# Throwaway matrix products behind a finished transformer kernel: 936 products from shifted places, with seven column counts

## The chip, the cores and the metric

The kernel runs on one core of a Trainium2 chip. The metric is the device time of one execution in microseconds (us). A core has five engines that run side by side, each through its own list of instructions: TensorE (PE: matrix products, with the loads of their weights on a line of their own, PEld), VectorE (DVE), ScalarE (ACT), GpSimd (POOL) and SyncE (SP, which here only issues DMAs). They meet through semaphores. SBUF is the memory that TensorE reads from, PSUM the one it writes to, in eight banks.

## What is computed

Two transformer blocks over 512 tokens of 1024 features. The first has two gated feed-forward layers around a mixer of short convolution and gated linear attention, the second has neighbourhood attention, a retention layer and a feed-forward layer of width 4096. Cut to its outline:

```python
def first_block(x, ...):
    x = x + FFN_RES_WEIGHT * swiglu(rmsnorm(x, norm_ffn1_g[l]), ffn1_w_gu[l], ffn1_w_down[l])
    x = x + hybrid_mixer(rmsnorm(x, norm_mix_g[l]), w_in[l], conv_w[l], ...)
    x = x + FFN_RES_WEIGHT * swiglu(rmsnorm(x, norm_ffn2_g[l]), ffn2_w_gu[l], ffn2_w_down[l])
    return rmsnorm(x, final_norm_g)

def second_block(x, ...):
    ...
    x = x + mix @ w_out[l]
    h = rms_norm(x, norm_mlp[l])
    x = x + jnp.square(jax.nn.relu(h @ w_up[l])) @ w_down[l]
    return rms_norm(x, norm_final)
```

The output is the normed result, 512 x 1024 float32 values.

## The kernel before

The program is written engine by engine, with every semaphore wait by hand. Features lie on the 128 partitions, tokens along the free dimension. A large product is made of **units**: 128 output features by 512 tokens, summed over eight (or six) blocks of 128 input features. Each float32 operand is split in a high and a low part of type float32r, and each block takes three products: high weights by high data, high weights by low data, low weights by high data (L2064 to L2066 in `unit`). Some layers work on half the tokens at a time, with combined operands (`pair`, L2156 to L2158): these have 256 columns. TensorE reads the data (the moving operand, up to 512 columns) and the weights (128 columns) from SBUF.

The tiles that matter lie one behind the other in each partition of SBUF. `X` starts at byte 16512. `Hhi`, `Hlo`, `Ahi` and `Alo` (L304 to L307, 16 KB each: eight blocks of 512 float32r values) follow at bytes 32896, 49280, 65664 and 82048, then `raw`, `wh` and `wl` (12 KB each) at 98432, 110720 and 123008. All of these addresses are 128 bytes past a multiple of 1024. `BThi` and `BTlo` (28 KB each, seven by four blocks of 256 values) lie in a region `M` that starts at byte 162880, which is 64 bytes past a multiple of 1024, and `BTlo` starts 28 KB behind it, so again 64 bytes past one. `H*` and `A*` hold activations, `wh` and `wl` the split weights of the units in work (three slots of 1024 values each), `BK[i]` is PSUM bank i.

The end of the program is written out by hand in `pe_program` behind L2534. The last unit is made in two halves of 256 tokens (`products`, L2538 to L2540), while the two other engines form the mean squares of the last norm (`sums`, one-column products, L2544). Eight groups of four transposes (`turned`, L2550) turn the normed result back so that tokens lie on the partitions. DVE scales one half of each token block out of PSUM (L2022) and counts the semaphore `esd` up, ACT scales the other half (L1128) and counts `esa`. Each of the four token blocks gives one `esd` and one `esa`. SP issues the output DMAs as these counts rise (L486, L489), ACT the last one (L1141), and SP then waits until all eight have landed. At the end of the block all engines meet.

Of the kernel before, what the change touches and what calls it, by code (L numbers as in the profile page):

```python
# [14 lines left out]
P = 128  # L15
# [276 lines left out]
def build(nc, dr, out):  # L292
    at = [int(nc.sbuf_base)]

    def sb(name, shape, dt=F32, off=None):
        nb = 4 * int(np.prod(shape[1:]))
        if off is None:
            off = (at[0] + 31) // 32 * 32
            at[0] = off + nb
        t = nc.alloc_sbuf_tensor_at(name, list(shape), dt, offset=off)  # L300
        return t, off

    X, _ = sb("X", [P, KT, T])
    Hhi, oHhi = sb("Hhi", [P, KT, T], F32R)  # L304
    Hlo, oHlo = sb("Hlo", [P, KT, T], F32R)
    Ahi, oAhi = sb("Ahi", [P, KT, T], F32R)
    Alo, oAlo = sb("Alo", [P, KT, T], F32R)  # L307
    RAWS, _ = sb("raw", [P, NRAW, 1024])
    WHS, _ = sb("wh", [P, NW, 1024], F32R)
    WLS, _ = sb("wl", [P, NW, 1024], F32R)  # L310
# [63 lines left out]
    BTlo, _ = sb("BTlo", [P, NP, 4, 256], F32R, off=M + 28 * KB)  # L374
# [4 lines left out]
    BK = [PS[:, i, :] for i in range(8)]  # L379
# [73 lines left out]
    s = {}  # L453
# [2139 lines left out]
        turned(3, 1)  # L2593


    ctx = ExitStack()
    with ctx:
        s.update({n: ctx.enter_context(nc.semaphore(f"s_{n}")) for n in SEMS})
# [134 lines left out]
```

## Time and profile before

| | |
|---|---|
| median time of 2 runs | 1753.58 us (1753.15 to 1754.0) |
| span of the profiled execution, first to last instruction | 1751.3 us |
| PE busy | 1744.0 us (100%), 10407 products |
| PEld, weight loads | 1534.4 us (88%) |
| DVE busy | 1238.9 us (71%) |
| ACT busy | 850.4 us (49%) |
| read from HBM | 170.70 MB |
| mean granted TensorE clock | 0.999 |

Times in the profile count from the start of the span. A row of the timeline gives start, length, engine, source line, operation, the output and input tiles, and how many like instructions stand in the row. Products are pipelined, and the length shown for one contains its way through the array, so that neighbouring rows overlap: the pace of a stream is read from the distance of the starts, not from the length.

### The profile page before, as it was taken

Reading aid. Unit: us, or ns where it says so; the run is one execution under the profiler, and the core shown is the slowest. Engines: PE = TensorE matmul, PEld = TensorE weight load, DVE = VectorE, ACT = ScalarE, POOL = GpSimd, SP = SyncE. Lnnn points to the kernel's source line nnn. Section 1 sums busy time; section 2 is a strip of 40 time slices with the busy share of each in tenths; the row PEclk is TensorE's granted clock in tenths of the full one; section 3 lists DMA queues with packets and bytes.
Section 4 is the critical chain, followed back from the end, with each engine's and each line's share of the span. In section 5 each row is a group of like instructions: output and inputs, shape, how many; then the busy total and the mean of one; then the engine's idle time right before and its main releaser. Section 6 shows DMA issues by size and latency. Waiting matters only on the chain.

```text
span 1751.3 us, 26596 instructions
## 1 busy us (share of the span) xinstructions
PE 1744.0 (100%) x10407; PEld 1534.4 (88%) x10407; DVE 1238.9 (71%) x1955; ACT 850.4 (49%) x1442; POOL 38.8 (2%) x38
## 2 busy tenths in 40 slices
PE   9999999999999999999999999999999999999998
PEld 7889989878888899988888998988877888989897
DVE  7949849666776557965795894976688677748474
ACT  6425526454333335743553562654655543627274
POOL 0000000000000000000000000000232000000000
PEclk9999999999999999999999999999999999999999
DMA  5232423332123232333323233334511233333232
GB/s 185 82 109 97 127 89 104 110 110 85 51 86 106 86 108 97 109 111 98 96 88 117 93 110 96 109 109 131 141 61 61 85 96 97 97 96 118 89 120 72
DMA packets 68427, 176.61 MB, mean 101 GB/s; under 512 B 8112, under 2 KB 9392, under 8 KB 68304
## 3 DMA queue, kind: packets, MB, share of 16 engines
q1 hardware_dynamic: 66576, 171.60, 31.4%
q10 hardware_dynamic: 1280, 2.08, 0.3%
q8 instruction: 83, 1.36, 0.3%
q0 software_dynamic: 448, 1.24, 0.3%
q14 instruction: 40, 0.33, 0.1%
HBM read 170.70 MB, written 2.10 MB: 99 GB/s over the span
## 4 chain that ended last, share of the span: by engine, by line
PE 95%; DVE 3%; ACT 1%; issue 1%; DMA 0%; DVEq 0%; ACTq 0%; POOLq 0%
PE ps L2064 18%; PE ps L2066 18%; PE ps L2065 18%; PE ps L2156 10%; PE ps L2158 10%; PE ps L2157 10%; PE ps L2086 2%; PE ps L2087 2%; PE ps L2088 2%; DVE wl L1159 1%; PE ps L2305 0%; ACT BThi L579 0%; PE ps L2435 0%; DVE BTlo L1231 0%; PE ps L2460 0%
## 5 line engine op out<-in xcount | busy, mean ns | idle before, releaser
L2064 PE MATMUL ps<-Ahi,wh 128*128 128x512 f32 x913 | 357.2, 391 | 0.0
L2065 PE MATMUL ps<-Alo,wh 128*128 128x512 f32 x913 | 355.4, 389 | 0.0
L2066 PE MATMUL ps<-Ahi,wl 128*128 128x512 f32 x913 | 355.4, 389 | 0.0
L2156 PE MATMUL ps<-BThi,wh 128*128 128x256 f32 x1232 | 340.6, 276 | 0.3 <-ACT tm L569 0.3
L2157 PE MATMUL ps<-BTlo,wh 128*128 128x256 f32 x1232 | 340.3, 276 | 0.0
L2158 PE MATMUL ps<-BThi,wl 128*128 128x256 f32 x1232 | 340.2, 276 | 0.0
L543 ACT ACTIVATE wh<-raw 128x1024 fp32r<-128x1024 f32 (+1 forms) x206 | 213.1, 1036 | 221.6 <-PE ps L2066 187.4
L1159 DVE TENSOR_TENSOR wl<-raw,wh 128x1024 fp32r<-128x1024 f32 (+1 forms) x206 | 250.1, 1215 | 64.6 <-ACT wh L543 62.6
L2156 PEld LDWEIGHTS ps<-BThi,wh 128*128 128x128 f32 x1232 | 231.3, 188 | 0.6 <-issue 0.6
L2157 PEld LDWEIGHTS ps<-BTlo,wh 128*128 128x128 f32 x1232 | 231.3, 188 | 0.0
L2158 PEld LDWEIGHTS ps<-BThi,wl 128*128 128x128 f32 x1232 | 231.3, 188 | 0.0
L2066 PEld LDWEIGHTS ps<-Ahi,wl 128*128 128x128 f32 x913 | 171.4, 188 | 35.8
L2064 PEld LDWEIGHTS ps<-Ahi,wh 128*128 128x128 f32 x913 | 171.4, 188 | 35.7 <-issue 0.2
L2065 PEld LDWEIGHTS ps<-Alo,wh 128*128 128x128 f32 x913 | 171.4, 188 | 35.5 <-issue 0.2
L2064 PE MATMUL ps<-Hhi,wh 128*128 128x512 f32 x494 | 195.8, 396 | 0.0
L2066 PE MATMUL ps<-Hhi,wl 128*128 128x512 f32 x494 | 192.5, 390 | 0.0
L2065 PE MATMUL ps<-Hlo,wh 128*128 128x512 f32 x494 | 192.4, 390 | 0.0
L553 ACT ACTIVATE wh<-raw 128x512 fp32r<-128x512 f32 x168 | 105.2, 626 | 58.2 <-PE ps L2066 40.2
L1166 DVE TENSOR_TENSOR wl<-raw,wh 128x512 fp32r<-128x512 f32 x168 | 114.8, 683 | 2.7 <-ACT wh L553 1.6
L553 ACT ACTIVATE wh<-SS 128x512 fp32r<-128x512 f32 x112 | 70.7, 631 | 85.8 <-DVE SS L1182 78.2
L2064 PEld LDWEIGHTS ps<-Hhi,wh 128*128 128x128 f32 x494 | 92.8, 188 | 22.0 <-issue 3.1
L2066 PEld LDWEIGHTS ps<-Hhi,wl 128*128 128x128 f32 x494 | 92.7, 188 | 19.6
(355 smaller groups left out, 2707.7 us busy)
## 6 DMA issues: line engine op xcount, KB each, us to landing
raw<-in_w_gu SPq DMA_DIRECT2D x128, 256.0 KB, 2.8
raw<-in_w_d SPq DMA_DIRECT2D x32, 512.0 KB, 3.5
raw<-in_w_dn SPq DMA_DIRECT2D x32, 512.0 KB, 3.8
raw<-in_w_up SPq DMA_DIRECT2D x48, 256.0 KB, 2.8
raw<-in_w_gu SPq DMA_DIRECT2D x22, 512.0 KB, 3.6
raw<-in_w_d SPq DMA_DIRECT2D x16, 384.0 KB, 3.1
raw<-in_w_v SPq DMA_DIRECT2D x8, 512.0 KB, 3.8
raw<-in_w_cc SPq DMA_DIRECT2D x8, 512.0 KB, 3.6
```

The costliest lines, as they stand in the source:

```text
L543: act.activation(WH[WS[u]][:, 0:n], RAW[RSL[u]][:, 0:n], ACT.Copy).then_inc(s["wh"], 1)
L553: act.activation(WHP[WS[p][c]], part(p, c), ACT.Copy).then_inc(s["wh"], 1)
L1159: dve.tensor_tensor(WL[WS[u]][:, 0:n], RAW[RSL[u]][:, 0:n], f32(WH[WS[u]][:, 0:n]), ALU.subtract).then_inc(s["wl"], 1)
L1166: dve.tensor_tensor(WLP[i], part(p, c), f32(WHP[i]), ALU.subtract).then_inc(s["wl"], 1)
L2064: pe.matmul(ps, wh[:, c], hi[:, k, :], start=(k == 0), stop=False)
L2065: pe.matmul(ps, wh[:, c], lo[:, k, :], start=False, stop=False)
L2066: last = pe.matmul(ps, wl[:, c], hi[:, k, :], start=False, stop=(k == nb - 1))
L2086: pe.matmul(ps, Hhi[:, k, tc], wh[:, c], start=(k == 0), stop=False)
L2087: pe.matmul(ps, Hlo[:, k, tc], wh[:, c], start=False, stop=False)
L2156: pe.matmul(ps, whi[:, w], bhi, start=(new and kp == 0), stop=False, skip_group_check=not new)
L2157: pe.matmul(ps, whi[:, w], blo, start=False, stop=False, skip_group_check=not new)
L2158: last = pe.matmul(ps, wlo[:, w], bhi, start=False, stop=(kp == 3), skip_group_check=not new)
```

## The change

Behind the last transposes TensorE gets one more piece of program. It waits until DVE and ACT have scaled all four blocks (`esd` and `esa` at 4), and then runs `shifted` 78 times. Each call makes four times three products into the first n columns of PSUM bank 0, with the kernel's order of high and low parts. `at` and `step` say where in the flat moving tile the columns start (`at + step * n * k`), `at_w` where the 128 weight columns start. Nothing reads what these products leave in the bank. The output is not touched. No other engine's program changes, and nothing ahead of this piece changes.

```diff
@@ -2593,6 +2593,51 @@
         turned(3, 1)
 
 
+        def shifted(n, moving, at, weights, at_w, step=1, same=False):
+
+            hi, lo = ((t[:, :, :].rearrange("p a b -> p (a b)") if len(t.shape) == 3 else
+                       t[:, :, :, :].rearrange("p a b c -> p (a b c)")) for t in moving)
+            wh, wl = (t[:, :, :].rearrange("p a b -> p (a b)") for t in weights)
+            for k in range(4):
+                m, c = at + step * n * k, at_w + (0 if same else P * k)
+                for i, (w, x) in enumerate(((wh, hi), (wh, lo), (wl, hi))):
+                    pe.matmul(BK[0][:, 0:n], w[:, c:c + P], x[:, m:m + n], start=(k == 0 and i == 0),
+                              stop=(k == 3 and i == 2))
+
+        pe.wait_ge(s["esd"], 4)
+        pe.wait_ge(s["esa"], 4)
+        H, A, B, W, HW = (Hhi, Hlo), (Ahi, Alo), (BTlo, BTlo), (WHS, WLS), (Ahi, Alo)
+        for i in range(3):
+            shifted(512, H, 0, W, 0)
+        for at in (0, 1, 2, 4, 8, 12, 16, 20, 24, 32, 40, 48, 64, 80, 96, 112, 128, 192, 256, 384):
+            shifted(512, H, at, W, 0)
+        for at in (4, 8, 16, 32, 48, 64, 96):
+            shifted(512, H, 0, W, at)
+        for at in (8, 16, 32, 64):
+            shifted(512, H, at, W, at)
+        for at in (0, 16, 48, 112, 240):
+            shifted(512, B, at, W, 0)
+        shifted(512, A, 0, W, 0)
+        shifted(512, A, 16, W, 0)
+        shifted(512, H, 0, W, 0, 1, True)
+        shifted(512, H, 16, W, 0, 1, True)
+        shifted(512, H, 0, HW, 0)
+        shifted(512, H, 16, HW, 0)
+        shifted(512, H, 0, (Hhi, Hlo), 2048)
+        for at in (0, 4, 8, 16, 24, 32, 48, 64, 128):
+            shifted(256, H, at, W, 0)
+        for at in (0, 8, 16, 32, 48, 240):
+            shifted(256, H, at, W, 0, 2)
+            shifted(256, B, at, W, 0)
+        for at in (0, 16):
+            shifted(384, H, at, W, 0)
+            shifted(448, H, at, W, 0)
+            shifted(320, H, at, W, 0)
+            shifted(128, H, at, W, 0)
+            shifted(480, H, at, W, 0)
+        shifted(512, H, 0, W, 0)
+
+
     ctx = ExitStack()
```

On TensorE, at the end of its program, the order before the change is this (four transposes of `X` stand in each pair of rows; the last row is the jump to the place where all engines meet):

```order
L2550 MATMUL ps<-ident,X 128x128 [waits s_eacc,s_ex]
L2550 MATMUL ps<-ident,X 128x128 x3
L2550 MATMUL ps<-ident,X 128x128 [waits s_esd]
L2550 MATMUL ps<-ident,X 128x128 x3
L2597 UNCONDITIONAL_BRANCH
```

With the change the same place on TensorE reads as follows (output tile, then the moving tile and the weight tile, then partitions by columns):

```order
L2550 MATMUL ps<-ident,X 128x128 [waits s_esd]
L2550 MATMUL ps<-ident,X 128x128 x3
L2604 MATMUL ps<-Hhi,wh 128x512 [waits s_esa,s_esd]
L2604 MATMUL ps<-Hlo,wh 128x512
L2604 MATMUL ps<-Hhi,wl 128x512
```

The jump has moved behind 936 products, of which only the first waits for anything.

The list of TensorE now ends with the twelve products of the last call and the jump:

```order
L2604 MATMUL ps<-Hlo,wh 128x512
L2604 MATMUL ps<-Hhi,wl 128x512
L2604 MATMUL ps<-Hhi,wh 128x512
L2604 MATMUL ps<-Hlo,wh 128x512
L2604 MATMUL ps<-Hhi,wl 128x512
L2642 UNCONDITIONAL_BRANCH
```

By columns, the 936 products are 564 of 512 (47 calls), 252 of 256 (21 calls), and 24 each of 480, 448, 384, 320 and 128 (two calls each). Together they have 395,520 columns.

## Rows read from the trace of the kernel before

**Rows 1.** The page's head, its busy times, and its forty slices.
```profile
span 1751.3 us, 26596 instructions
...
PE 1744.0 (100%) x10407; PEld 1534.4 (88%) x10407; DVE 1238.9 (71%) x1955; ACT 850.4 (49%) x1442; POOL 38.8 (2%) x38
...
PE   9999999999999999999999999999999999999998
...
PEclk9999999999999999999999999999999999999999
```

**Rows 2.** The page's chain that ended last, by engine.
```profile
PE 95%; DVE 3%; ACT 1%; issue 1%; DMA 0%; DVEq 0%; ACTq 0%; POOLq 0%
```

**Rows 3.** Timeline around the end: start, length, engine, line, operation.
```profile
1744.23 2.38 PE L2550 MATMUL ps<-ident,X 128*128 128x128 f32 x20
...
1745.85 1.41 DVE L2022 TENSOR_SCALAR OT<-ps,rt 128x512 f32<-128x512 f32 x2
...
1746.28 1.26 ACT L1128 ACTIVATE OT<-ps,rt 128x512 f32<-128x512 f32 x2 [0.26 <-PE ps L2550]
...
1747.51 0.46 SPq L486 DMA_DIRECT2D out<-OT  x1
1747.57 0.36 ACTq L1141 DMA_DIRECT2D out<-OT  x1
```

**Rows 4.** Waits of the DMA queue of SP, 1742 to 1752 us.
```profile
SPq L2597 <- DMA out<-OT: 3.0, 1, 3.0
```

**Rows 5.** Timeline of PE at 566 us, 512 columns, first and last of 25.
```profile
566.21 0.39 PE L2064 MATMUL ps<-Ahi,wh 128*128 128x512 f32 x1
566.44 0.39 PE L2065 MATMUL ps<-Alo,wh 128*128 128x512 f32 x1
...
571.65 0.39 PE L2064 MATMUL ps<-Ahi,wh 128*128 128x512 f32 x1
```

**Rows 6.** Timeline of PE at 1115 us, 256 columns from BThi/BTlo, first and last of 37.
```profile
1114.77 0.28 PE L2158 MATMUL ps<-BThi,wl 128*128 128x256 f32 x1
...
1118.85 0.28 PE L2158 MATMUL ps<-BThi,wl 128*128 128x256 f32 x1
```

**Rows 7.** Timeline of PE at 1736 us, 256 columns from Ahi/Alo, first and last of 27.
```profile
1735.83 0.28 PE L2538 MATMUL ps<-Ahi,wh 128*128 128x256 f32 x1
...
1738.95 0.28 PE L2540 MATMUL ps<-Ahi,wl 128*128 128x256 f32 x1
```

**Rows 8.** Groups of PE by line and shape: count, busy us, mean ns.
```profile
L2064 PE MATMUL ps<-Ahi,wh 128*128 128x512 f32 x913 | 357.2, 391 | 0.0
...
L2064 PE MATMUL ps<-Hhi,wh 128*128 128x512 f32 x494 | 195.8, 396 | 0.0
...
L2550 PE MATMUL ps<-ident,X 128*128 128x128 f32 x32 | 3.9, 274 | 0.0
```

**Rows 9.** PE by stretches: length, PE busy (products), granted clock, DMA share, GB/s.
```profile
1742.56:1746.61 4.05, 4.05 (x38) 1.00 0.42 161
1746.61:1747.70 1.09, 0.01 (x1) 1.00 1.01 378
1746.61:1751.30 4.69, 0.01 (x1) 0.75 0.82 308
```

**Rows 10.** Timeline of PE at the program's start.
```profile
1.06 4.23 PE L2323 MATMUL ps<-ones 128*128 128x256 f32 x10 [1.06 <-DVE ones L1558]
```

**Rows 11.** Timeline of PE at 421 us.
```profile
421.36 1.46 PE L2293 MATMUL ps<-VT,KST 128*128 128x256 f32 x6
```

## The prediction

> **What bounds the kernel now.** I read the page's head first. TensorE is busy in 1744.0 of 1751.3 us, in every one of the forty slices, at the full granted clock [rows 1]. The chain that ended last is 95% TensorE [rows 2]. So the kernel is bound by the stream of products, and anything put into that stream lengthens it. The change puts its products behind the stream, so next I read the end of the timeline, for what may cover them.
>
> The last transposes end at 1746.61 (1744.23 + 2.38). DVE's last scaling ends at 1747.26 and ACT's at 1747.54, and the last two output DMAs are issued at 1747.51 and 1747.57 [rows 3]. SP then waits 3.0 us for the output to land [rows 4], and the span closes at 1751.3. In this stretch of some 3.7 us TensorE has nothing to do. That is all the cover there is.
>
> Last I read the pace of like products, from the distance of the starts. 512 columns: (571.65 - 566.21) / 24 = 0.2267 us each [rows 5]. 256 columns out of `BThi`/`BTlo`: (1118.85 - 1114.77) / 36 = 0.1133 us [rows 6]. 256 columns out of `Ahi`/`Alo`: (1738.95 - 1735.83) / 26 = 0.1200 us [rows 7]. The reader is to see two things. Between the 256 and the 512 columns of the A tiles lie 0.1067 us, which is one column per tick of 2.4 GHz, the level that a granted clock of 1.00 stands for. And each product pays something on top of its columns: 0.0133 us out of the A tiles, 0.0067 us out of the B tiles. The A tiles lie 128 bytes past a multiple of 1024, the B tiles 64 bytes past one. So the place of the data may change a product's price already in this kernel, by 0.0067 us. The calls of the change vary that place.
>
> **What the change removes, adds and moves.** Nothing is removed or moved: every row ahead of the new piece is the same on all engines. Added are two waits and 936 products, each with its own weight load. No DMA is added, and nobody waits for these products except the meeting of all engines at the end.
>
> *Start.* The wait for `esd` costs nothing by itself; the wait for `esa` ends last, with ACT's end at 1747.54. SP's DMA is issued 0.25 us after the DVE instruction that it waits for (1747.26 to 1747.51), so I let the first product start 0.16 us after ACT, at 1747.7; between 0.05 and 0.3 us the difference is nothing here.
>
> *The 564 products of 512 columns.* The same operation with the same operands as the kernel's own [rows 8], whose pace is 0.2267. Twenty-one of the 47 calls read from the kernel's own places or from ones a multiple of 128 bytes away; the others are shifted by 64 bytes more or by less than that. I can bound a shifted one from below by its columns alone, 0.2133, as in the last paragraph, and above by a product that pays twice the A tiles' surcharge, 0.2400, if reads that don't start on a round address take one more step. Between the two I take 0.226, a little under the A pace, since some calls shift into the place of the B tiles: 564 x 0.226 = 127.5 us. Bounds: 120.3 and 135.4 us.
>
> *The 252 products of 256 columns.* Fifteen of the 21 calls read `H`, which lies as the A tiles do, six read `B`, and shifts bring each into the other's place: 0.1200 and 0.1133 are both at hand, I take 0.116: 29.2 us. Bounds 0.1067 and 0.1333: 26.9 and 33.6 us.
>
> *The 24 each of 480, 448, 384 and 320 columns.* By the line through the A tiles' two paces (0.0133 + columns / 2400): 0.2133 + 0.2000 + 0.1733 + 0.1467 = 0.7333 us, times 24 = 17.6 us. Bounds 16.3 and 18.9 us.
>
> *The 24 of 128 columns.* The line would give 0.067 us. No row of the kernel shows a float32r product so short; the nearest is the transpose of 128 columns, twenty of them in 2.38 us with the way through the array [rows 3, 8], (2.38 - 0.27) / 19 = 0.111 us. A product that short may wait for its weights, which are 128 columns too. I take 0.11: 2.6 us; with 0.053 it is 1.3 us.
>
> Sum: 127.5 + 29.2 + 17.6 + 2.6 = 176.9 us. By the lower bounds 164.8 us, by the upper ones 190.5 us.
>
> *End.* The last product still needs its way through the array, about 0.16 us (a length of 0.39 less the pace of 0.23 [rows 5]), and then the engines meet. Before, that took from the landing (1747.97 + 3.0 = 1750.97) to 1751.3, 0.33 us. The output has landed long before, so the 3.0 us of its wait, which were the path of the end, drop out and are not paid.
>
> Span after: 1747.7 + 176.9 + 0.16 + 0.33 = **1925.1 us**. The median of the runs shown is 2.3 us above the span of the profiled execution (1753.58 - 1751.3), and the work around the span does not change: **1927.4 us**, 9.9% more than before. Put otherwise, 176.9 us of products, less 3.4 us that they share with the output's landing and the drain, plus the drain of their own.
>
> The notes state another pace. The Trainium skill, page "TensorE: Matmul & The Clock Gate", section "Back-to-back issue gap", gives a full-clock gap of columns / 2.4 GHz plus 2.5 ns for a single product, some 216 ns for 512 columns. By it the whole addition would be about 167 us and the time about 1918 us, an estimate from that page. The kernel's own rows are 11 ns above it at 512 columns, and the measurement decides.
>
> **The clock.** TensorE stands idle from 1746.61 to about 1747.7, and the granted clock in these 1.09 us is 1.00. Over the whole idle stretch to 1751.3 it is 0.75, so it fell to 0.5 (the 1.2 GHz level) about half way, near 1749.0, after some 2.3 us without work [rows 9]. With the change the idle time ends after 1.1 us. I cost the clock at nothing in the sum.
>
> **The rivals.**
>
> *The clock drops once at the start of the new piece* (0.12). For it: it did drop in this very stretch, if later, and before the gap there were only transposes and one-column products for 4 us. Against: it was at 1.00 all through these and the 1.1 us behind them. Price: at the program's start ten products take 4.23 us [rows 10], 0.42 us each; six of the same type and columns later take 1.46 us, under 0.25 us each with the last one's way through the array [rows 11]. That is a stretch of about 4 us at half pace, after which the pace is full, so one such stretch costs some 2 us: 1929.5 us. The skill's same page, section "Part 4: PE-mode transpose", holds that transposes don't count as work in the way that products do. By it this rival would be the likelier case; the clock of 1.00 through 4.05 us of transposes speaks against it so far.
>
> *Reads from odd places cost much more* (0.08). If a start that is no multiple of 64 bytes made each product take twice its time, this would hit eleven of the 512-column calls (shifts of the data by 1, 2, 4, 8, 12, 20, 24 or 40 values, of the weights by 4 or 8, and of both by 8) and five of the 256-column ones: 132 x 0.2267 + 60 x 0.117 = 37 us more, 1964 us. If only starts off a multiple of 16 bytes did (shifts of 1 and 2), 24 x 0.2267 = 5.4 us more, 1933 us. Nothing in the profile is for it, since the kernel has no such read, and nothing is against it.
>
> *Shifted and shorter products run at the price of their columns* (0.06): 164.8 us of products in the place of 176.9, 1915.3 us. For it: the B tiles' surcharge is only half of the A tiles'. Against: no stream of float32r products in the kernel pays less than 0.0067 us.
>
> *The products do not reach the end: the time is not slower* (0.01). For this the addition would have to fit into the 3.7 us of idle time and 2% of the kernel, 35 us: under 39 us for 936 products, 0.041 us each, where the 512-column ones alone would have to stream their columns at five times the pace seen. It could only be if the products were left out, and the order of instructions has all 936 of them ahead of the jump to the meeting of the engines. Then it would be 1753.6 us.
>
> *The clock falls and stays down* (0.02), with 353.8 us of products: about 2104 us. The dense stream of 1744 us at 1.00 speaks against it.
>
> The forecast itself has the rest, 0.71, with its own range of 1920 to 1933 us.
>
> **How the numbers follow.** The predicted time is that of the likeliest case, 1927.4 us. The range has to leave out no more than 2 in 10 and take in the bounds of the unknown paces: 164.8 us of products gives 1915, 190.5 us gives 1941. The odd-place case at its dearest and the clock that stays down lie outside, with under 0.1 together. So 1915 to 1941. A measurement of this kernel can tell about 2% from no change (35 us); all cases but the one without products lie over 9% above. Slower by over 2%: 0.99; within 2%: 0.01; faster: 0.
>
> **What would show it.** In the profile after, everything up to 1747.5 us has its old times. A row of L2604 with 936 products follows, starting near 1747.7. The starts lie 0.227 us apart in the first 36 products, where nothing is shifted; if they lie 0.45 apart at first, the clock has dropped. The shifted calls lie within 0.213 to 0.240; a call with 16 values' shift at 0.220 would say that 64 bytes are what separates the A tiles' price from the B tiles'. SP's wait for the output is followed by one for TensorE of about 170 us. The prediction is wrong if shifts move the pace by more than a few per cent, if products of 128 columns are not near 0.11 us, or if a call's first product, which opens a new sum in the same bank, waits for the one before.

## The result, and the profile after

| | before | after |
|---|---|---|
| median time | 1753.58 us (2 runs) | 1930.26 us (2 runs, 1930.21 and 1930.3) |
| ratio | | 1.1008, 95% interval 1.0987 to 1.1029 |
| span of the profiled execution | 1751.3 us | 1928.4 us |
| forecast | | 1927.4 us, range 1915 to 1941 |

The change makes the kernel 10.1% slower, by 176.7 us. The page of the changed kernel has the busy products of TensorE grown by 936 and everything else as it was (compare [rows 1]):

```profile
span 1928.4 us, 28469 instructions
...
PE 1924.6 (100%) x11343; PEld 1689.5 (88%) x11343; DVE 1239.4 (64%) x1955; ACT 850.5 (44%) x1442; POOL 38.7 (2%) x38
```

Its timeline around the end of the old program (to compare with [rows 3]): start, length, engine, line, operation.

```profile
1744.19 2.38 PE L2550 MATMUL ps<-ident,X 128*128 128x128 f32 x20
...
1746.23 1.27 ACT L1128 ACTIVATE OT<-ps,rt 128x512 f32<-128x512 f32 x2 [0.26 <-PE ps L2550]
...
1747.53 0.36 ACTq L1141 DMA_DIRECT2D out<-OT  x1
...
1747.64 0.47 PE L2604 MATMUL ps<-Hhi,wh 128*128 128x512 f32 x1 [1.07 <-ACT OT L1128]
...
1927.78 0.39 PE L2604 MATMUL ps<-Hhi,wl 128*128 128x512 f32 x1
```

The piece starts 0.14 us after ACT's last end (1747.50), and its last product starts at 1927.78: 935 distances in 180.13 us. The waits of SP's queue now name TensorE where [rows 4] named the output (longest wait last in the row):

```profile
SPq L2642 <- PEq L2642: 175.5, 1, 175.5
```

Stretches of this trace in the form of [rows 9] (length, PE busy with its products, clock, DMA share, GB/s), the first at the program's start, the second about the gap, the third nearly all of the piece:

```profile
0.00:4.00 4.00, 2.94 (x7) 1.00 0.52 160
...
1746.50:1747.60 1.10, 0.07 (x1) 1.00 1.02 382
...
1747.60:1925.00 177.40, 177.36 (x923) 1.00 0.02 7
```

The clock column says nothing here. This trace holds no record of the granted clock, and the column prints 1.00 for the first 4 us too, in which the row of ten slow products from [rows 10] runs (4.32 us here). So the clock has to be read from the pace. The first distances of the piece are 306, 235 and 234 ns, and they settle at 227. A piece that starts at the 1.2 GHz level shows 592, 427 and 427 (further below, in an execution whose trace has the record). The clock did not fall here.

The paces come out of the timeline of TensorE after. The first rows here are the starts of the calls with shifts of the data of 0, 1 and 2 values, the last three those of the calls on `BTlo` with shifts of 0, 16 and 48:

```profile
1755.93 0.39 PE L2604 MATMUL ps<-Hhi,wh 128*128 128x512 f32 x1
...
1758.65 0.40 PE L2604 MATMUL ps<-Hhi,wh 128*128 128x512 f32 x1
...
1761.51 0.40 PE L2604 MATMUL ps<-Hhi,wh 128*128 128x512 f32 x1
...
1841.80 0.39 PE L2604 MATMUL ps<-BTlo,wh 128*128 128x512 f32 x1
...
1844.60 0.39 PE L2604 MATMUL ps<-BTlo,wh 128*128 128x512 f32 x1
...
1847.34 0.40 PE L2604 MATMUL ps<-BTlo,wh 128*128 128x512 f32 x1
```

Twelve products lie between neighbouring rows of a pair. Unshifted: (1758.65 - 1755.93) / 12 = 0.2267 us. Shifted by one value: 2.86 / 12 = 0.2383. `BTlo` as it lies: 2.80 / 12 = 0.2333. `BTlo` shifted by 16 values: 2.74 / 12 = 0.2283, and 0.2267 in its last seven. So place counts, and at 512 columns the B tiles' place is the dearer one, the reverse of [rows 6, 7] at 256. By columns, all of the piece:

| columns | products | measured us each | forecast us each | difference of the sums, us |
|---|---|---|---|---|
| 512 | 563 distances | 0.2308 | 0.226 | +2.7 |
| 256 | 252 | 0.1179 | 0.116 | +0.5 |
| 480 | 24 | 0.2216 | 0.2133 | +0.2 |
| 448, 384, 320 | 72 | 0.2031, 0.1744, 0.1465 | 0.2000, 0.1733, 0.1467 | +0.1 |
| 128 | 24 | 0.1073 | 0.11 | -0.1 |

### The profile page after: what moved, and what is told of

It reads as the page before. It is cut to its first block, busy times and chain, and to the rows that moved or that the text cites. A ratio compares the mean times of both kernels' runs of the same rounds, so it can differ in the third digit from the quotient of the medians.

```text
span 1928.4 us, 28469 instructions
## 1 busy us (share of the span) xinstructions
PE 1924.6 (100%) x11343; PEld 1689.5 (88%) x11343; DVE 1239.4 (64%) x1955; ACT 850.5 (44%) x1442; POOL 38.7 (2%) x38
## 3 DMA queue, kind: packets, MB, share of 16 engines
q1 hardware_dynamic: 66576, 171.60, 28.3%
## 4 chain that ended last, share of the span: by engine, by line
PE 95%; DVE 3%; ACT 1%; issue 1%; DMA 0%; DVEq 0%; ACTq 0%; POOLq 0%
PE ps L2064 16%; PE ps L2065 16%; PE ps L2066 16%; PE ps L2604 9%; PE ps L2156 9%; PE ps L2158 9%; PE ps L2157 9%; PE ps L2086 2%; PE ps L2088 2%; PE ps L2087 2%; DVE wl L1159 1%; PE ps L2305 0%; ACT BThi L579 0%; PE ps L2435 0%; DVE BTlo L1231 0%
## 5 line engine op out<-in xcount | busy, mean ns | idle before, releaser
L2158 PEld LDWEIGHTS ps<-BThi,wl 128*128 128x128 f32 x1232 | 231.2, 188 | 0.0
L553 ACT ACTIVATE wh<-raw 128x512 fp32r<-128x512 f32 x168 | 105.1, 625 | 58.1 <-PE ps L2066 40.2
L2065 PEld LDWEIGHTS ps<-Hlo,wh 128*128 128x128 f32 x494 | 92.8, 188 | 19.5 <-issue 1.0
```

What stands on the lines that cost most here:

```text
L553: act.activation(WHP[WS[p][c]], part(p, c), ACT.Copy).then_inc(s["wh"], 1)
L2065: pe.matmul(ps, wh[:, c], lo[:, k, :], start=False, stop=False)
L2158: last = pe.matmul(ps, wlo[:, w], bhi, start=False, stop=(kp == 3), skip_group_check=not new)
```

## The experiments

Unless it says otherwise, an experiment is the changed kernel with another piece at its end, run once with its profile; what differs is far below the 2% that single times tell, so the distances of the starts within the profile decide, and the times are beside them. The front of the program varies by up to 1.3 us between executions (the last twenty transposes start at 1744.13 in one and 1745.42 in another), so I compare from there.

### Is it the shifts, or the calls?

```diff
-        for i in range(3):
-            shifted(512, H, 0, W, 0)
-        for at in (0, 1, 2, 4, 8, 12, 16, 20, 24, 32, 40, 48, 64, 80, 96, 112, 128, 192, 256, 384):
-            shifted(512, H, at, W, 0)
...
+        for n, count in ((512, 46), (256, 21), (384, 2), (448, 2), (320, 2), (128, 2), (480, 2), (512, 1)):
+            for i in range(count):
+                shifted(n, H, 0, W, 0)
```

> The same 936 products with the same column counts, all read from the start of Hhi/Hlo and wh/wl (no shift of data or weights, no other tiles). Theory PLACE (a product's price follows from where its data lie relative to its weights): 512 columns at 0.2267 throughout, 256 columns at 0.1200, 564 x 0.2267 + 252 x 0.1200 + 20.2 = 178.3 us of products instead of the 180.1 us seen with the shifts, time 1928.4 us. Rival CALL (each call costs something when it opens a new sum in the same bank, whatever the place): as with the shifts, 180.1 us and 1930.3 us, and slower products at the head of each call of twelve.

Measured: 1929.43 us, span 1927.6 us, 178.56 us from the first start to the last (forecast 178.3, with the shifts 180.13). The distances are 227, 226, 227 ns in every call of 512 but the first and the last, over every call's head, and 120 ns in every call of 256 after the first. So a new sum in the same bank costs nothing, and the shifts cost 1.6 us in all: 2.2 us more in the products of 512 columns (127.8 us unshifted, 129.9 shifted) and 0.5 us less in those of 256 (30.2 and 29.7). Only the first eleven products after a change are irregular: 306, 235, 233, 236, 224, 231, 236, 228, 233, 231, 226, and then 227.

### What the cover of the idle time is worth

```diff
-        pe.wait_ge(s["esd"], 4)
-        pe.wait_ge(s["esa"], 4)
...
-                pe.matmul(BK[0][:, 0:n], w[:, c:c + P], x[:, m:m + n], start=(k == 0 and i == 0),
+                pe.matmul(BK[END[5]][:, 0:n], w[:, c:c + P], x[:, m:m + n], start=(k == 0 and i == 0),
```

> The changed kernel without the two waits ahead of the piece, its products going into the bank of the first transposes, which has been read by then. The piece starts right behind the last transposes, at 1746.6 instead of 1747.64. Theory: the piece is added end to end to the stream, so the time falls by the whole gap, 1.0 to 1.1 us, to 1929.2 us, and the slow products at the head of the piece (306, 235, 234 ns apart) are at 227. Rival: something else holds the start (the fetch of the new instructions), and the time stays at 1930.3 us.

Measured: 1929.64 us, span 1927.8 us. In its timeline the piece follows the transposes without a gap:

```profile
1744.93 2.38 PE L2550 MATMUL ps<-ident,X 128*128 128x128 f32 x20
1747.07 0.47 PE L2604 MATMUL ps<-Hhi,wh 128*128 128x512 f32 x1
1747.38 0.39 PE L2604 MATMUL ps<-Hlo,wh 128*128 128x512 f32 x1
```

From the start of the transposes to the end of the span it is 182.9 us, after the change 184.2 us: 1.3 us less, of which the gap is 1.07; the rest is that the first product now starts 0.24 us before the last transpose has come through the array (1744.93 + 2.38 = 1747.31). The piece is simply put end to end with the stream, as the forecast had it. Its slow head stays (the distances are 314, 229, 233, 236, 224, 231, 236), so that is no effect of the gap; the expectation was wrong there, and what makes the head stays open.

### What the clock would have cost

```diff
+        pe.wait_ge(s["out"], 128)
         pe.wait_ge(s["esd"], 4)
         pe.wait_ge(s["esa"], 4)
```

> The changed kernel with one more wait of TensorE ahead of the piece: it starts when the output has landed, near 1751.1 us, after some 4.5 us without work instead of 1.07. Theory CLOCK (the granted clock falls about 2.3 us into the idle stretch, as it did before the change, and comes back after some 4 us of work): 3.5 us later start plus about 2 us at half pace, 1930.3 + 5.5 = 1935.8 us, and starts about 0.45 us apart in the first products. Rival: the clock does not matter here, 1933.8 us and 0.227 us apart from the first product on.

Measured: 1936.67 us, span 1934.8 us. The stretches of TensorE, with the columns as above:

```profile
1747.00:1752.70 5.70, 0.00 (x0) 0.66 0.65 240
1752.70:1755.50 2.80, 2.75 (x7) 0.50 0.00 0
1755.50:1760.00 4.50, 4.50 (x21) 0.99 0.00 0
```

And the first rows of the piece in the timeline:

```profile
1752.75 0.79 PE L2604 MATMUL ps<-Hhi,wh 128*128 128x512 f32 x1 [5.99 <-DMA out<-OT]
...
1753.34 0.63 PE L2604 MATMUL ps<-Hlo,wh 128*128 128x512 f32 x1
...
1753.77 0.63 PE L2604 MATMUL ps<-Hhi,wl 128*128 128x512 f32 x1
```

After 6.0 us without work the clock is at the 1.2 GHz level, the products are 0.427 us apart, and after seven of them the clock is back. Counted from the last transposes, the piece starts 4.9 us later than in the changed kernel (8.38 us behind their start instead of 3.45), 1.4 us more than I had taken, and it lasts 181.46 us instead of 180.13. The fall therefore cost 1.3 us; I had expected 2. In the changed kernel the gap of 1.07 us cost no clock.

### Which place, and of what

```diff
+        run(512, 0, 0)
+        for x in range(4, 68, 4):
+            run(512, x, 0)
+        for x in range(8, 72, 8):
+            run(512, 0, x)
+        for x in (16, 32, 48):
+            run(512, x, x)
+        for x in range(0, 68, 4):
+            run(256, x, 0)
+        for x in (16, 32, 48):
+            run(256, 0, x)
```

`run(n, x, w)` makes 24 products of n columns in the kernel's order, with the data shifted by x values and the weights by w.

> In the place of the 78 calls, runs of 24 like products each: 512 columns with the data shifted by 0 to 64 values in steps of 4, with the weights shifted by 8 to 64 in steps of 8, with both shifted by 16, 32 and 48; then 256 columns with the data shifted by 0 to 64 in steps of 4 and the weights by 16, 32 and 48. Theory PLACE: only the difference data minus weights counts, and it repeats every 64 values (256 bytes). So 0 and 64 give 0.2267, both shifted alike give 0.2267, the weights shifted by 16 give what the data shifted by 48 give (0.2333), by 48 what 16 give (0.229), both by 32 give 0.2328; at 256 columns 0.1200 at difference 0, 0.1133 at 48, 0.118 at 16 and 32. Rival ADDRESS (the data's own address decides): weight shifts change nothing (0.2267), and data shifted along with the weights costs as data shifted alone.

Measured: 1962.11 us (the piece is longer). The mean distance of the starts over the last twelve products of each run, in ns, by the difference data minus weights in values, modulo 64 (that is 256 bytes):

| difference | 0 | 8 | 16 | 24 | 32 | 40 | 48 | 56 |
|---|---|---|---|---|---|---|---|---|
| 512 columns, data shifted | 226.7 | 233.3 | 228.9 | 233.3 | 232.6 | 234.3 | 233.3 | 233.3 |
| 512 columns, weights shifted | 226.6 | 232.7 | 228.8 | 233.6 | 233.5 | 233.5 | 233.4 | 233.2 |
| 256 columns, data shifted | 120.0 | 116.7 | 117.8 | 120.0 | 119.0 | 117.2 | 113.3 | 118.3 |
| 256 columns, weights shifted | | | 117.8 | | 118.8 | | 117.9 | |

With the data shifted by 4, 12, 20, 28, 36, 44, 52 and 60 values, 512 columns take 231.7, 233.3, 231.1, 231.1, 233.3, 233.3, 235.0 and 226.7 ns. With both shifted by 16, 32 or 48 values they take 226.6 ns. Rows from its timeline show three shifts by 32 values. The data shifted, a run of 24: (1797.69 - 1792.11) / 24 = 0.2325 us. The weights shifted: (1864.65 - 1859.05) / 24 = 0.2333 us. Both shifted, the last twelve: (1897.76 - 1895.04) / 12 = 0.2267 us.

```profile
1792.11 0.40 PE L2602 MATMUL ps<-Hhi,wh 128*128 128x512 f32 x1
...
1797.69 0.40 PE L2602 MATMUL ps<-Hhi,wh 128*128 128x512 f32 x1
...
1859.05 0.40 PE L2602 MATMUL ps<-Hhi,wh 128*128 128x512 f32 x1
...
1864.65 0.39 PE L2602 MATMUL ps<-Hhi,wh 128*128 128x512 f32 x1
...
1895.04 0.39 PE L2602 MATMUL ps<-Hhi,wh 128*128 128x512 f32 x1
...
1897.76 0.39 PE L2602 MATMUL ps<-Hhi,wh 128*128 128x512 f32 x1
```

What follows: at 512 columns the difference alone decides, to within 1 ns, and no place of those tried is better than the kernel's own, 0 (60 values, 16 bytes short of the next 0, gives the same 226.7); the data's address by itself explains nothing, since it can be shifted for nothing if the weights go along. At 256 columns the order is another one, with the best at a difference of 48 values, where `B*` lie in the kernel, and also at 28 (113.3). One point does not fit: at 256 columns a difference of 48 made by moving the weights gives 117.9, made by moving the data 113.3. It is no proof against the difference either, because the same read can have two paces. In the changed kernel the data shifted by 48 values, with 512 values from block to block, gave 117.5; the run here reads the very same addresses and gave 113.3. Nor is it the 12 products of a call against the 24 of a run. Unshifted products of 256 columns with 32 weight columns appear in two later experiments, from the same addresses: 24 of them behind products of 256 columns are (1772.73 - 1770.01) / 24 = 0.1133 us apart, 90 of them behind products of 512 columns (1858.82 - 1848.22) / 90 = 0.1178 us, from the first to the last.

```profile
1770.01 0.28 PE L2602 MATMUL ps<-Hhi,wh 128*32 128x256 f32 x1
...
1772.73 0.22 PE L2602 MATMUL ps<-Hhi,wh 128*128 128x128 f32 x1
```

```profile
1848.22 0.28 PE L2605 MATMUL ps<-Hhi,wh 128*32 128x256 f32 x1
...
1858.82 0.40 PE L2605 MATMUL ps<-Hhi,wh 128*128 128x512 f32 x1
```

So at 256 columns a stream from the same addresses can keep either of two paces, 4.5 ns apart. What differed between the two, besides the execution and the length of the stream, was what ran ahead of it; that this is the cause is argued and not shown, and how it would act stays open. The single values of the table at 256 columns are to be read with that in mind.

### The same, in the kernel itself

If the place is the cause, it must show in the 4272 products of `pair` that read `B*` and `MT*`, without any piece at the end. Three versions of the kernel before, timed in three rounds each beside it (1753.77 us, median of 7 runs), differ in one number. With 192 the pairs lie at a difference of 0 from their weights, with 64 at 32 values, with 256 at 16:

```diff
-    M = (at[0] + 31) // 32 * 32 + 128
+    M = (at[0] + 31) // 32 * 32 + 192
```

> The kernel before, without the new piece, with the region M placed 64 bytes later, so that BThi/BTlo and MThi/MTlo lie at difference 0 from the weights (modulo 256 bytes) instead of 192. Theory PLACE: their 4272 products of 256 columns cost 0.1200 instead of 0.1133, 4272 x 0.0067 = 28.5 us more, plus 0.5 us for the 192 of MG*, 1782.5 us. Rival ADDRESS or TILE (what was seen belongs to the tiles or to the piece at the end): 1753.6 us.

> The kernel before with M 64 bytes earlier: pairs at difference 128. Theory PLACE: 256 columns at 0.1185 to 0.1195, 22 to 26 us more, plus 1.3 us for the 192 products of MG*, about 1778 us. Rival: 1753.6 us.

> The kernel before with M 128 bytes later: pairs at difference 64. Theory PLACE: 256 columns at 0.1177 to 0.1180, 19 to 20 us more, about 1774 us. Rival: 1753.6 us.

| difference of the pairs, values | time, us | ratio to before (95%) | expected, us | BThi and BTlo products, mean ns apart |
|---|---|---|---|---|
| 48 (before) | 1753.77 | | | 113.7 |
| 0 | 1781.36 | 1.0158 (1.0143 to 1.0173) | 1782.5 | 120.1 |
| 32 | 1776.34 | 1.013 (1.0113 to 1.0147) | about 1778 | 118.8 |
| 16 | 1773.26 | 1.0112 (1.0097 to 1.0127) | about 1774 | 117.9 |

From the timeline of the version with difference 0, first and last of 35 rows, to compare with [rows 6]: (1118.52 - 1114.44) / 34 = 0.1200 us instead of 0.1133.

```profile
1114.44 0.28 PE L2158 MATMUL ps<-BThi,wl 128*128 128x256 f32 x1
...
1118.52 0.28 PE L2156 MATMUL ps<-BThi,wh 128*128 128x256 f32 x1
```

A shift of a memory region by 64 bytes costs this kernel 27.6 us. That is under 2%, but the interval of the ratio leaves 1 well outside. The shift moves every tile of `M`, not only those of the pairs; by the distances of the starts, TensorE's stream is 28.3 us longer in the profile, and 26.9 us of that lie in the 4272 products of the pairs. The same sum is 21.5 of 23.4 us for the version with 32 and 17.8 of 20.3 us for the one with 16. In these versions only the data move, so they show that the place of the data counts at 256 columns, and not by themselves that it counts relative to the weights. The changed kernel, with all its calls, showed of this effect only 1.6 us.

### Where does the surcharge come from? First try: fewer weights

> In the place of the 78 calls, runs of 24 like products, unshifted: 512, 256, 128 and 64 columns, each with 128, 64 and 32 weight columns; 512 columns into two banks in turn, and 512 with each product a sum of its own; 256 and 512 columns shifted by 48 and 32 values with fewer weight columns; then fourteen column counts from 496 to 96. Theory COLLISION (the surcharge comes from the weight load that runs beside a product and gets in the way of its data): it shrinks with the weights, 512 columns cost 0.2267 with 128 weight columns, 0.220 with 64 and 0.2167 with 32; short products wait for their weights, 128 columns cost 0.11, 0.06 and 0.055 with 128, 64 and 32 weight columns; banks and sums make no difference. Rival FIXED (handling per product, or opening and adding in the same bank): 0.2267 with any weight columns; if it is the bank, 0.2133 to 0.22 with two banks in turn.

The piece was `run` with 512, 256, 128 and 64 columns, each with 128, 64 and 32 weight columns, and the variants that the text names. Measured (1876.2 us), distances in ns over the last twelve products:

| columns | 128 weight columns | 64 | 32 |
|---|---|---|---|
| 512 | 226.6 | 229.8 | 231.8 |
| 256 | 120.2 | 113.3 | 113.3 |
| 128 | 111.7 | 59.9 | 60.1 |
| 64 | 111.7 | 58.3 | 53.3 (at the 1.2 GHz level; 32.1 at full clock, see below) |

The rows at the start of three runs, 512 columns with 64 weight columns and then with 32, give the same: (1758.83 - 1753.31) / 24 = 0.2300 and (1764.39 - 1758.83) / 24 = 0.2317 us.

```profile
1753.31 0.40 PE L2602 MATMUL ps<-Hhi,wh 128*64 128x512 f32 x1
...
1758.83 0.40 PE L2602 MATMUL ps<-Hhi,wh 128*32 128x512 f32 x1
...
1764.39 0.28 PE L2602 MATMUL ps<-Hhi,wh 128*128 128x256 f32 x1
```

Theory COLLISION falls as I had put it: at 512 columns fewer weights make the unshifted product dearer, not cheaper. It is not out altogether, for elsewhere fewer weights do make it cheaper: 120.2 to 113.3 ns at 256 columns, and with the data shifted by 32 values 512 columns take 233.8, 229.7 and 231.2 ns with 128, 64 and 32 weight columns. Two banks in turn (once the clock was back) and a sum for every product give 226.7, so the rival with the bank falls too. What holds is the floor: below some 256 columns a float32r product waits for its 128 weight columns, 111.7 ns whatever its own columns (224, 192, 160, 128 and 96 columns all gave 111.6 to 111.9).

### Second try: let the data stand still

Two lines of the new helper make the operand one column, read again and again:

```diff
+                xs = mt[:, m:m + 1].broadcast_to([P, n]) if one_x else mt[:, m:m + n]
+                ws = wt[:, c:c + 1].broadcast_to([P, cols]) if one_w else wt[:, c:c + cols]
```

> What is the surcharge of 0.0133 us at equal places? Fewer weight columns did not shrink it. In the place of the 78 calls, runs of 24 products, unshifted: 512 and 256 columns whose data are one column repeated (read in place, not running through memory); the same with one weight column repeated 128 times; both; 512 columns with the same block of data and weights each time; 256 columns into the second half of the bank; plain float32 (two passes) with 512, 256 and 128 columns; bfloat16 with 256, 128 and 64 columns; float32r again with 128 and 64 columns. Theory READ (two reads, of data and of weights, that run through memory side by side get in each other's way): with the data standing still 512 columns cost 0.2157 or less, and 256 columns 0.109; with only the weights standing still a little less than 0.2267. Rival PIPE (float32r products have a fixed changeover between products that is rounded up to a step of 16 columns): 0.2267 and 0.1133 to 0.1200 whatever is read. Either way 64-column float32r products at 0.1117 with 128 weight columns, and if the weights' width in bytes sets that floor, bfloat16 at 64 columns near 0.056.

Measured (1837.65 us), ns apart: 512 columns as usual 226.7; one data column repeated 215.8; one weight column repeated 231.1; both 215.8; the same blocks each time 226.7; 256 columns with one data column repeated 111.7, which is the floor of the weights; with one weight column repeated 113.3; into the second half of the bank 120.1, as into the first. Plain float32 makes two rows of each product, which start 429.2, 215.8 and 111.7 ns apart for 512, 256 and 128 columns. bfloat16 109.2, 55.8 and 29.2 for 256, 128 and 64 columns, where float32r takes 111.7 for both 128 and 64. The rows at the start and the end of the first still run, (1759.12 - 1753.94) / 24 = 0.2158 us:

```profile
1753.94 0.38 PE L2605 MATMUL ps<-Hhi,wh 128*128 128x512 f32 x1
...
1759.12 0.27 PE L2605 MATMUL ps<-Hhi,wh 128*128 128x256 f32 x1
```

So 11 of the 13.3 ns of surcharge at 512 columns come with data that run through memory, and 2.5 ns are left without. Theory READ holds for the data. The other types bear on this: plain float32 has 2.5 ns per row on top of two ticks per column (1024 / 2.4 = 426.7), and bfloat16, read from a tile of ones, 2.5 ns on top of one (256 / 2.4 = 106.7). So the 11 ns appear in these runs only where four bytes per partition are read with every tick. For the weights the theory doesn't hold at 512 columns: with one weight column read 128 times over the product is dearer still (231.1), while at 256 columns it is cheaper (113.3 instead of 120.0). That the difference of the two addresses decides the price at 512 columns, and yet fewer or standing weights raise it there and lower it at 256, I cannot bring under one mechanism; it stays open. The 2.5 ns agree with the Trainium skill, page "TensorE: Matmul & The Clock Gate", section "Back-to-back issue gap" (columns / 2.4 GHz plus 2.5 ns, 215.8 for 512). Its section "LDWEIGHTS (loading the stationary operand)" gives columns / 1.2 GHz, 107 ns for 128 weight columns and 53 for 64: the floors of 111.7 and 58.3 ns are 5 ns above that. For bfloat16 the floor is gone (29.2 ns), in line with the same page's "Weight-path perf modes", by which weights are read 32 bits at a time, a gain for bfloat16 and none for float32.

### The clock in a stream of short products

> In the run with fewer weight columns the granted clock fell to the 1.2 GHz level inside an unbroken stream, while 64-column products with 32 weight columns ran. Here six streams of some 10 us each (columns by weight columns: 64x32, 64x64, 64x128, 128x32, 256x32, 512x32) stand between runs of 45 full products (512x128). Theory ACTIVITY (a stream without gaps whose products use a small part of the array counts as little work): the clock falls in 64x32 and in others with few weight columns, rises again in the full products behind them, and stays at 1.00 in 64x128, though that stream has the same 64 columns. Rival CHANCE (the fall was an event of its own): 1.00 throughout. Times at 1.00: 0.053 or less, 0.058, 0.1117, 0.060, 0.1133, 0.2318 us per product.

Measured (1893.04 us). The stretches of TensorE for the streams of 64 columns with 32, 64 and 128 weight columns (the last in two parts), then of the full products behind it, then of 128 columns with 32 weight columns:

```profile
1759.20:1768.80 9.60, 9.60 (x301) 1.00 0.02 3
1779.20:1789.00 9.80, 9.80 (x171) 1.00 0.01 2
1799.40:1802.60 3.20, 3.20 (x32) 1.00 0.02 5
1802.70:1815.40 12.70, 12.70 (x62) 0.50 0.00 0
1815.40:1819.60 4.20, 4.20 (x11) 0.50 0.00 0
1819.70:1827.70 8.00, 8.00 (x36) 1.00 0.00 0
1827.80:1837.90 10.10, 10.10 (x171) 1.00 0.01 3
```

This trace has the record of the clock. The expectation is turned round. The clock fell in the one stream that I had taken as safe, 64 columns with full weights, without a gap and with 111.7 ns from start to start, and it stayed down through the rest of it and 4.3 us into the full products behind. At the 1.2 GHz level these 64-column products were 213.3 ns apart, so the floor of the weights (111.7 at full clock) nearly doubles when the clock halves. In the streams with few weight columns, where 64-column products follow each other in 32.1 and 58.1 ns, the clock stayed at 1.00, and also in those of 128, 256 and 512 columns with 32 weight columns (60.0, 117.8 and 231.7 ns; the second was expected at 113.3). The fall in the run with fewer weight columns came at about 1782.4, some 1.5 us behind 24 products of 64 columns with full weights; it may belong to those and not to the ones that ran when it came, but with one such case that is only argued. The two 128-column calls of the changed kernel, 1.3 us each, did not bring the clock down.

## Why the prediction was right, and where it was off

**The bound and the place.** The forecast that the piece is added end to end behind a stream that is itself the bound holds: taking its waits away gave 1.3 us for a gap of 1.07.

**Start.** 1747.7 forecast, 1747.64 seen. The first eleven distances are irregular where I had taken 0.227 from the start, which costs 0.1 us.

**The 564 products of 512 columns.** The term that was mis-sized: 0.2308 us instead of 0.226, 2.7 us of the 3.4 by which the products came out dearer. The step that failed is that shifts would bring some calls "into the place of the B tiles" and so under the A pace. I had carried the B tiles' small surcharge from 256 to 512 columns. At 512 columns that place costs 0.2333, and no shift was under 0.2267. The sign that I had named for it, 0.220 at a shift of 16 values, did not come: it was 0.229. I had also counted places a multiple of 128 bytes away as the kernel's own, and at 128 bytes 512 columns cost 0.2326; the period is 256 bytes. How near the total came is in part luck: the shifts raised the 512-column products by 2.2 us and lowered those of 256 columns by 0.5 us, and 1.9 us of the miss stand without any shift, for the unshifted piece takes 178.56 us where I had 176.7 from first to last start. The upper bound of 0.2400 held: the dearest, by one value, took 0.2383, 5% over the unshifted pace, which is at the edge of the "few per cent" that I had named as the sign of being wrong.

**The 252 of 256 columns.** 0.1179 instead of 0.116, 0.5 us, between the two rows that were at hand, and nearer to the dearer. With 120.0 for the unshifted ones the shifts did lower this term, as forecast, but by half as much.

**480 to 320 columns.** The line through 256 and 512 held for 384 and 320, and was 3 ns low at 448 and 8 ns at 480, where the first product behind the 128-column ones also waits 0.27 us.

**128 columns.** 0.1073 instead of 0.11, and 0.1117 in a steady run. The row of transposes was the right neighbour, and waiting for the weights is the reason: with half the weight columns it is 0.060.

**End and offset.** The time of the profiled execution lies 1.8 us above its span (1930.21 - 1928.4). The 2.3 us of the forecast set the median of two executions against the span of one of them; against the faster of the two it is 1.8 as well (1753.15 - 1751.3). So the span came out 3.3 us above the forecast (3.4 in the products), and half a us came back in this slip: 2.9 us in all.

**The clock.** Costed at nothing, and by the pace it did not fall. The price that I gave the rival, some 2 us, was 1.3 when the gap was made long enough. The rule that I had drawn from the Trainium skill's "Part 4: PE-mode transpose" (page "TensorE: Matmul & The Clock Gate"), that transposes don't count as work, did not show here: in seven executions with the transposes and up to 1.07 us of gap the clock stayed up, by its record in three of them and by the pace of the products in the other four.

**Odd places.** The rival of doubled reads is out: one value's shift costs some 11 ns in 226.7, not twice the time, and four values' 5.

## What to carry to other kernels

Read a pace from the distance of the starts at the shape and place you need: a surcharge seen at 256 columns need not hold at 512. In a kernel bound by float32r products, the place of the data relative to the weights modulo 256 bytes is worth a sweep: 64 bytes in one allocation made 1.6% here. And a clock column of 1.00 is worth checking against a stretch that is known to be slow, before it is read as full speed. Products of fewer than about 256 columns wait for their 128 float32r weight columns (0.112 us), and work behind a bound stream costs its full length, less only the idle time at the end.

## What the runs showed of the hardware that was not expected

- The price of a float32r product of 512 columns follows the difference of the data's and the weights' addresses: 226.7 ns at 0, 228.9 at 64 bytes, 232.6 to 234.3 at the other multiples of 32 bytes, 226.7 once more at 240 bytes, 238 with the data 4 bytes off, repeating every 256 bytes. At 256 columns the best is 113.3 at 192 and 112 bytes, the worst 120.0, and the same read can keep 113.3 or 117.8 through a whole stream.
- A stream falls into a regular pattern only after some ten products: 306, 235, 233, 236, 224, 231, 236, 228, 233, 231, 226 and then 227 ns.
- With the data standing still a 512-column product takes 215.8 ns. Plain float32 and bfloat16 pay the same 2.5 ns on top of their ticks with running data, so the other 11 ns were seen only at four bytes per tick.
- The floor of 111.7 ns for 128 float32r weight columns is 213.3 ns at the 1.2 GHz level.
- The clock fell to the 1.2 GHz level inside an unbroken stream of 64-column products with 128 weight columns, 3.3 us after its start, and not in streams of the same columns with 64 or 32 weight columns.
